# A two-layer decoder step on one core: the border between the layers in eight column steps, with the next layer's first tile among them

## The chip, the core and the metric

The kernel runs on one core of one Trainium2 chip. The metric is the device time of one execution in microseconds (us); lower is better. Before the change the median of three runs was 2055.4 us (2051.17 to 2055.42). The engines are named as the profile names them: PE is TensorE, PEld its weight loads, DVE VectorE, ACT ScalarE, POOL GpSimd, SP SyncE.

## The reference, cut to what matters

A prompt of 512 tokens behind 16 meta tokens and 8 sample tokens (536 rows in all) go through two layers of width 2048. Layer 0 has a pooling mixer and differential attention, layer 1 has gated linear attention with four heads. Each layer has the same frame:

```python
z = rms_norm(h, pre_g) @ w_in
...
h = h + rms_norm(mix @ w_out, post_g)
```

So the border between the layers needs, in this order: the last product of `mix @ w_out` of layer 0; the sum of squares over the whole row of 2048; the scaled residual `h`; its transposition, since PE wants the 2048 columns on the partitions; and `rms_norm(h, pre_g) @ w_in` of layer 1. The kernel multiplies `pre_g` into the transposed rows and applies the row's own `1/rms` only after the products, so the products of layer 1 needn't wait for the second norm.

Everything is float32. A product of two float32 matrices is made of three PE products of rounded parts ("hi" and "lo"): lo x hi, hi x lo, hi x hi.

## The kernel before, in words

**Engines and order.** Each engine has a program of its own, written out by hand, in order; semaphores tie them together. Weights stream through two raw buffers `wraw` (half a tile, 512 KB, each): SP loads a chunk (`load`, L451, and `out_load`, L531), ACT rounds it into `whi` (`split`, L663), POOL subtracts to get `wlo` (`lo`, L598), PE multiplies. SP may load a chunk only when POOL is done with the one two before it, and its program is in order: a wait in it holds up every load behind it.

**Layer 0** is four pairs of attention heads (`pair` on each engine), 24 weight chunks each. The programs of PE and DVE are written out for all four; those of SP (pairs 1 to 3, L528), POOL (L621) and ACT (pairs 0 to 2, L833) are loops of the chip with addresses in registers. Pages of the key and value caches are fetched by SP (`fetch`, L481), the last two samples' values by ACT (L773).

**Output products** (`out_stage` on each engine; once per layer). 32 chunks of weights; four column blocks of 512, each over eight chunks; per chunk PE makes 24 products for the four row tiles of 128 (`out_stage`, L1113). The last 24 rows (the tail) are made apart by narrow products straight from the raw weights (`tail_group`, L1098), copied to SBUF by DVE (L1785), and folded together by one product behind the block (L1140 to 1142). ACT squares every block's tile into a partial sum (`square`, L864), the tail last; DVE multiplies it by the post-norm weights `gain` (L1788, L1790). `gain` is loaded by SP behind chunk 9 (L543 to L547), after waits for ACT's last copy of the activations and for DVE. Before chunk 2 POOL has made the activations' residues (`lows`, L633) and the tails' copies (`mix_tails`, L624), and ACT the activations' copies (`mix_hi`, L711). When the products end, ACT first splits the first two chunks of layer 1 (L855), then squares the last block; DVE adds the sums (L1792), behind its multiply of the tail; ACT makes Ln and Exp (L861).

**The border** (L881 on ACT, L1320 on PE, L1797 to L1827 on DVE) goes in four steps of 512 columns. DVE makes five residuals, one for each row tile (L1800); PE transposes the 512 columns into four banks (`row_transposes`), ACT copies them with `pre_g` as the scale (L884), DVE makes the low parts (`low_rows`); PE multiplies the columns by 16 low-rank columns of `w_in` (`low_rank`, L1335). Behind the four steps ACT issues the stores of `h` (L888 to L890), squares `h` row by row over 2048 columns (L893), and makes the next norm; DVE puts it on diagonals (L1831), PE spreads it (`spread_rstd`), DVE copies it and scales the low-rank rows (L1841).

**Layer 1** is four heads (`head` on each engine), 24 chunks each: four value tiles, two of queries, two of keys, four of gates. The first chunk of the first value tile is multiplied ahead of PE's spread of the norm (L1440 to L1442), the second behind it. SP loads the decay weights `wa2` behind chunk 2 of a head, after a wait for the low-rank rows (L571 to L575). PE and the last head of ACT and DVE are written out; the first three heads of ACT (L1022) and DVE (L2020) and all heads of SP and POOL are loops.

## Time and profile before

| what | before |
|---|---|
| median of three runs | 2055.4 us (2051.17 to 2055.42) |
| the profiled execution: its own time | 2051.26 us |
| its span, first to last instruction | 2049.5 us |
| PE busy | 1950.3 us (95%), 13625 products |
| DVE, ACT, POOL busy | 732.8, 643.2, 899.9 us |
| mean granted clock of PE | 0.97 |

The span is what the profiler saw of one execution; its own time is 1.8 us longer, which lies around the span. A busy PE is not PE at its peak: products overlap, and the clock it is granted is not always the higher one. A row of the timeline gives the start from the beginning of the span, the duration, the engine and line, what is written from what, how many instructions were put together, and in brackets how long the engine had been idle and what released it. Nearly all PE work shows line 1036 or 1039, which are helpers, so its rows are told apart by their tiles.

### The profile page before, as it was taken

How to read it: one execution, taken by the hardware profiler on the slowest of the kernel's cores; microseconds unless marked ns; L12 is line 12 of the kernel's file. 1: busy time of each engine (PE TensorE's matmuls, PEld its weight loads, DVE VectorE, ACT ScalarE, POOL GpSimd, SP SyncE). 2: the span in 40 equal slices, each digit the busy share in tenths (PEclk: the TensorE clock that was granted, in tenths of full speed). 3: DMA queues.
4: the chain of work that ended last, by engine and by line, in shares of the span. 5: the costliest groups of instructions: out<-in, count | busy, mean ns of one | idle time of the engine just before them, and what ended most of it. 6: DMA issues, size and time to landing. Idle time of an engine off the chain costs nothing.

```text
span 2049.5 us, 36126 instructions
## 1 busy us (share of the span) xinstructions
PE 1950.3 (95%) x13625; PEld 1724.1 (84%) x13625; DVE 732.8 (36%) x1439; ACT 643.2 (31%) x1186; POOL 899.9 (44%) x1196
## 2 busy tenths in 40 slices
PE   6999999999999999999889999999999999989996
PEld 6998999898979887677679988988998899867774
DVE  5245235425442556000251354044305522550003
ACT  6132223222221234222243253334334423442221
POOL 2464447345624654544314333433442444354442
PEclk9999999999999999999999999999999899989998
DMA  5454345434533442352233543445244424522422
GB/s 169 118 154 134 96 117 145 142 87 126 149 114 106 130 140 89 103 168 83 75 119 95 153 145 93 118 119 183 65 125 153 133 77 125 177 83 99 170 91 111
DMA packets 300100, 250.05 MB, mean 122 GB/s; under 512 B 14855, under 2 KB 258968, under 8 KB 297016
## 3 DMA queue, kind: packets, MB, share of 16 engines
q1 hardware_dynamic: 260256, 189.06, 31.4%
q10 hardware_dynamic: 39688, 58.83, 8.7%
q8 instruction: 108, 1.77, 0.4%
q14 instruction: 48, 0.39, 0.1%
HBM read 215.73 MB, written 32.57 MB: 121 GB/s over the span
## 4 chain that ended last, share of the span: by engine, by line
issue 45%; POOL 33%; PE 19%; DVE 1%; DMA 0%; POOLq 0%; ACT 0%; DVEq 0%; SPq 0%; ACTq 0%
POOL wlo L603 28%; PE proj L1036 9%; PE score L1036 5%; POOL kv L618 4%; PE scratch L1036 4%; POOL xlo L637 1%; PE proj L1039 0%; DVE mix L1800 0%; DMA xin<-in_x_prompt 0%; POOLq L601 0%; POOL mtail L631 0%; PE score L1039 0%; PE scratch L1039 0%; DVEq L168 0%; DVE ytail L1800 0%
## 5 line engine op out<-in xcount | busy, mean ns | idle before, releaser
L603 POOL TENSOR_TENSOR wlo<-wraw,whi 128x256 fp32r<-128x256 f32 x1032 | 777.3, 786 | 1101.7 <-ACT whi L667 1101.2
L1036 PE MATMUL proj<-xhi,wlo 128*128 128x268 f32 (+1 forms) x3104 | 910.5, 293 | 8.2 <-POOL wlo L603 8.1
L1036 PE MATMUL proj<-xlo,whi 128*128 128x268 f32 (+1 forms) x3104 | 897.0, 289 | 0.0
L1036 PE MATMUL proj<-xhi,whi 128*128 128x268 f32 (+1 forms) x3104 | 896.4, 289 | 0.0
L1036 PEld LDWEIGHTS proj<-xhi,wlo 128*128 128x128 f32 x3104 | 596.7, 192 | 25.1 <-issue 19.7
L1036 PEld LDWEIGHTS proj<-xlo,whi 128*128 128x128 f32 x3104 | 596.7, 192 | 0.7
L1036 PEld LDWEIGHTS proj<-xhi,whi 128*128 128x128 f32 x3104 | 595.1, 192 | 0.0
L667 ACT ACTIVATE whi<-wraw 128x1024 fp32r<-128x1024 f32 x258 | 268.1, 1048 | 674.8 <-PE proj L1036 290.1
L1464 DVE TENSOR_TENSOR tz<-proj,rstd 128x536 f32<-128x536 f32 (+1 forms) x72 | 51.2, 712 | 327.7 <-PE proj L1036 327.2
L1036 PE MATMUL proj<-wlo,xhi 128*128 128x512 f32 x256 | 102.8, 402 | 0.0
L1036 PE MATMUL proj<-whi,xhi 128*128 128x512 f32 x256 | 101.1, 395 | 0.0
L1036 PE MATMUL proj<-whi,xlo 128*128 128x512 f32 x256 | 101.1, 395 | 0.0
L618 POOL TENSOR_TENSOR kv<-kv,qb 128x256 f32<-128x256 f32 x128 | 93.0, 756 | 5.6 <-DMA kv<-in_cache_k 4.4
L753 ACT ACTIVATE probw<-score,small 128x128 f32<-128x128 f32 (+3 forms) x64 | 33.2, 523 | 162.8 <-DVE small L1559 162.8
L1036 PE MATMUL score<-wlo,xhi 128*128 128x512 f32 x160 | 65.3, 408 | 5.3 <-POOL wlo L603 5.3
L1036 PEld LDWEIGHTS proj<-wlo,xhi 128*128 128x128 f32 x256 | 48.3, 189 | 24.4 <-issue 11.7
L1036 PE MATMUL score<-whi,xlo 128*128 128x512 f32 x160 | 64.7, 404 | 0.0
L1036 PE MATMUL score<-whi,xhi 128*128 128x512 f32 x160 | 64.5, 403 | 0.0
L1940 DVE SCALAR_TENSOR_TENSOR sst<-vb,gk,sst 128x512 f32<-128x512 f32 x64 | 57.0, 950 | 8.2 <-ACT sst L954 7.4
L1036 PEld LDWEIGHTS proj<-whi,xlo 128*128 128x128 f32 x256 | 48.2, 188 | 11.3
L1036 PEld LDWEIGHTS proj<-whi,xhi 128*128 128x128 f32 x256 | 48.4, 189 | 10.9
L1785 DVE COPY te<-proj 128x512 f32<-128x512 f32 x4 | 2.8, 692 | 135.5 <-DMA gain<-in_post_norm 77.5
(311 smaller groups left out, 2088.6 us busy)
## 6 DMA issues: line engine op xcount, KB each, us to landing
wraw<-in_w_in SPq DMA_DIRECT2D x192, 512.0 KB, 4.0
wraw<-in_w_out SPq DMA_DIRECT2D x64, 512.0 KB, 4.6
kv<-in_cache_k SPq DMA_DIRECT2D x128, 128.0 KB, 2.2
sst<-in_state_gla ACTq DMA_DIRECT2D x32, 512.0 KB, 5.1
out<-sst ACTq DMA_DIRECT2D x32, 512.0 KB, 3.6
kv<-in_cache_v SPq DMA_DIRECT2D x96, 128.0 KB, 2.2
vb<-v_sample_rows ACTq DMA_DIRECT2D x32, 256.0 KB, 5.5
qb<-q_sample_rows SPq DMA_DIRECT2D x32, 128.0 KB, 3.3
```

Source lines behind the costliest of these rows:

```text
L603: last = pool.tensor_tensor(wlo[:, slot, k:k + 2, 0:width], wraw[:, kc, k:k + 2, 0:width], whi[:, slot, k:k + 2, 0:width].bitcast(F32), AL ...
L618: last = pool.tensor_tensor(kv[b % 2][:, pg, :], kv[b % 2][:, pg, :], qb[b % 2][:], ALU.mult)
L637: pool.tensor_tensor(xlo[:, p, :], mix[:, ORDER[which][p], :], xhi[:, p, :].bitcast(F32), ALU.subtract).then_inc(s_xp, 1)
L667: act.activation(whi[:, 2 * par + kc, :, 0:width], wraw[:, kc, :, 0:width], ACT.Copy).then_inc(s_hi, 1)
L753: last = act.activation(prob[:, m, 0:n], score2[:, m, 0:n], ACT.Exp, bias=small[:, 2 + m:3 + m], scale=SCALE, accum_out=small[:, 4 + m:5 + m])
L1036: return pe.matmul(out, lhsT, rhs, start=start, stop=stop, skip_group_check=True)
L1464: dve.tensor_tensor(dst, src, root, ALU.mult).then_inc(s_evac, 1)
L1785: dve.tensor_copy(tef[:, 0:BLK], blk_bank(which, 5 * nb + TT)).then_inc(s_tcopy, 1)
L1940: last = dve.scalar_tensor_tensor(out=sst[i][:, j, :], in0=vb[i][:], scalar=gk[:, j, TP + b:TP + b + 1], in1=sst[i][:, j, :], op0=ALU.mult ...
```

## The change

1. **The border has eight steps of 256 columns.** Three banks (`row_bank`) take the transposes. In each step PE makes the low-rank products of the step before and also that step's products of the first value tile (`first_tile`), into the other `proj` buffer; its two chunks, 0 and 1 of the first head, are left out there.
2. **The next norm's squares** are made by ACT piece by piece inside the border (512 columns, 20 pieces, behind every second step) and added by DVE. The three fills of DVE (L1837 to L1839) move ahead of the next norm.
3. **The stores of `h`** move from ACT to SP, behind chunk 3 of the first head, with a wait for the last residual; `wa2` of the first head is loaded behind them, without the wait for the low-rank rows.
4. **The fold of the tail** moves ahead of the block's last 24 products; ACT squares the tail first; DVE's sum over the partial squares stands ahead of its last multiply; of the splits behind the products, those of the first value tile move behind Ln and Exp.
5. **Norm weights**: SP loads `gain` behind chunk 3 instead of chunk 9, and DVE waits for it only at its first multiply.
6. **Start of the output products**: POOL makes `wlo` of chunks 2 and 3 ahead of its last four activation residues, ACT splits them ahead of its last eight copies.
7. **Loops written out**: `pair` and `head` on SP, POOL, ACT and DVE.

The diff, cut to its core:

```diff
+        def row_bank(k):
+            return banks[(4, 6, 7)[k % 3]]
...
-            with sp.Fori(1, PAIRS) as g:
+            for g in range(1, PAIRS):
                 pair(g)
...
-                    if q == 9:
+                    if q == 3:
...
-            def head(s):
+            def head(s, first=False):
                 for c in range(24):
                     load(N_HEAD + c // 2 + 12 * s, c % 2, w_in1, head_col(c // 2, s))
-                    if c == 2:
+                    if c == 3 and first:
+
+                        sp.wait_ge(s_x1, 5 * STEPS)
+                        sp.dma_start(h_dram[TT, 0:TB], ytok[TT]).then_inc(s_hst_tail, 16)
+                        for tt in range(TT):
+                            sp.dma_start(h_dram[tt], ytok[tt]).then_inc(s_hst, 16)
+                        sp.wait_ge(s_hst_tail, 16)
+                        sp.dma_start(wa2[:], A["gla_wa2_1"][:, 0:GK]).then_inc(s_wa2, 16)
+                    if c == 2 and not first:
                         src = A["gla_wa2_1"][:, bass.ds((s + 1) * GK - GK, GK)]
-                        sp.wait_ge(s_lr, 1)
                         sp.wait_ge(*freed_back("head", "G11", s))
                         sp.dma_start(wa2[:], src).then_inc(s_wa2, 16)
...
+                for c in range(2 * n0 + 2, 2 * n0 + 4):
+                    lo(c, c % 4)
                 lows(which, (9, 11, 13, 15))
-                for c in range(2 * n0 + 2, 2 * n0 + 32):
+                for c in range(2 * n0 + 4, 2 * n0 + 32):
                     lo(c, c % 4)
...
+                for c in range(2 * n0 + 2, 2 * n0 + 4):
+                    split(c // 2, c % 2, c // 2 % 2)
                 for p, sig_ready in ready:
                     if sig_ready:
                         act.wait_ge(*sig_ready)
                     mix_hi(which, (p, p + 1))
-                for c in range(2 * n0 + 2, 2 * n0 + 32):
+                for c in range(2 * n0 + 4, 2 * n0 + 32):
...
-                    if q % 8 == 3 and q > 3:
-                        tail_square(which, q // 8 - 1)
-                for c in last:
-                    split(c // 2, c % 2, c // 2 % 2, RANK if c < 2 * N_LR + 2 else P)
+                for c in last[0:2]:
+                    split(c // 2, c % 2, c // 2 % 2, RANK)
                 block_squares(which, NBLK - 1)
-                tail_square(which, NBLK - 1)
                 act.wait_ge(s_rsum, which + 1)
                 act.wait_ge(s_ya, 5 * NBLK * (which + 1))
                 chain.link(act.activation(row_sum, row_sum, ACT.Ln, scale=1.0 / D, bias=eps))
                 act.activation(row_rs, row_sum, ACT.Exp, scale=-0.5).then_inc(s_rs, 1)
+                for c in last[2:]:
+                    split(c // 2, c % 2, c // 2 % 2)
...
+            for e in range(STEPS):
+                for k in (2 * e, 2 * e + 1):
...
-                    act.activation(xhi[:, k, 0:TT * P], banks[(2, 3, 6, 7)[k % 4]], ACT.Copy,
+                    act.activation(xhi[:, k, 0:TT * P], row_bank(k), ACT.Copy,
                                    scale=cols[:, PRE1 + k:PRE1 + k + 1]).then_inc(s_mh, 1)
-                act.wait_ge(s_gt, c + 1)
-                act.activation(xhi[:, 4 * c:4 * c + 4, TT * P:T], te4(c), ACT.Copy).then_inc(s_gth, 1)
-            act.dma_start(h_dram[TT, 0:TB], ytok[TT]).then_inc(s_hst_tail, 16)
-            for tt in range(TT):
-                act.dma_start(h_dram[tt], ytok[tt]).then_inc(s_hst, 16)
-            for tt in range(TT + 1):
-                w = P if tt < TT else TB
-                last = act.activation(hbuf[tt][0:w], ytok[tt][0:w], ACT.Square, accum_out=rsum[0:w, 30 + tt:31 + tt])
-            chain.link(last)
+                act.wait_ge(s_gt, e + 1)
+                act.activation(xhi[:, 2 * e:2 * e + 2, TT * P:T], te2(e), ACT.Copy).then_inc(s_gth, 1)
+                for t in range(TT + 1) if e % 2 else ():
+                    c = e // 2
+                    i, w = 5 * c + t, P if t < TT else TB
+                    if i >= 2:
+                        act.wait_ge(s_nsq, i - 1)
+                    act.activation((tzf, rstdf)[i % 2][0:w, 0:BLK], ytok[t][0:w, c * BLK:(c + 1) * BLK], ACT.Square,
+                                   accum_out=rsum[0:w, 40 + t * NBLK + c:41 + t * NBLK + c]).then_inc(s_nsq, 1)
...
+                        if k0 == KT - 2:
+                            pe.wait_ge(s_tcopy, NBLK * which + nb + 1)
+                            matmul(blk_bank(which, 5 * nb + TT)[0:TB, :], tfold, tef[:, 0:BLK]).then_inc(s_blk, 1)
...
-                    if grp % 4 == 3:
-                        pe.wait_ge(s_tcopy, NBLK * which + nb + 1)
-                        matmul(blk_bank(which, 5 * nb + TT)[0:TB, :], tfold, tef[:, 0:BLK]).then_inc(s_blk, 1)
...
+            def row_transposes(e):
+                pe.wait_ge(s_x1, 5 * e + 5)
+                if e:
+                    pe.wait_ge(s_gt, e)
+                for k in (2 * e, 2 * e + 1):
                     last = transpose(banks[5][:, k * TB:(k + 1) * TB], ytok[TT][:, k * P:(k + 1) * P])
                 last.then_inc(s_xtt, 1)
...
+                for k in (2 * e, 2 * e + 1):
+                    if k >= 3:
+                        pe.wait_ge(s_ml, k - 2)
+                    for t in range(TT):
+                        last = transpose(row_bank(k)[:, t * P:(t + 1) * P], ytok[t][:, k * P:(k + 1) * P])
+                    last.then_inc(s_xtr, 1)
...
+            def first_tile(e):
+
+                pe.wait_ge(s_lo, 2 * N_HEAD + 3 + e // 4)
+                for k in (2 * e, 2 * e + 1):
+                    for a in range(2):
+                        slot, x = 2 + k // HC, slice(a * TH, (a + 1) * TH)
+                        out = proj[1][:, a, 0:TH]
+                        matmul(out, wlo[:, slot, k % HC, :], xhi[:, k, x], start=k == 0, stop=False)
+                        matmul(out, whi[:, slot, k % HC, :], xlo[:, k, x], start=False, stop=False)
+                        last = matmul(out, whi[:, slot, k % HC, :], xhi[:, k, x], start=False, stop=k == KT - 1)
+                if e == STEPS - 1:
+                    last.then_inc(s_tile, 1)
+
             row_transposes(0)
-            pe.wait_ge(s_evac, N_LR + 1)
+            pe.wait_ge(s_evac, N_LR + 2)
             pe.wait_ge(s_lo, 2 * N_LR + 4)
-            for c in range(1, 4):
-                row_transposes(c)
-                low_rank(c - 1)
-            low_rank(3)
+            for e in range(1, STEPS):
+                row_transposes(e)
+                low_rank(e - 1)
+                first_tile(e - 1)
+            low_rank(STEPS - 1)
+            first_tile(STEPS - 1)
+            spread_rstd(2)
...
-                    chunk(n0 + c // 2, (1 + c // 2) % 2, c % 2, *((META, QH) if HEAD_TILES[c // 2][0] in "qg" else (0, TH)))
-                    if s == 0 and c == 0:
-                        spread_rstd(2)
+                    if s or c >= 2:
+                        chunk(n0 + c // 2, (1 + c // 2) % 2, c % 2, *((META, QH) if HEAD_TILES[c // 2][0] in "qg" else (0, TH)))
...
-                dve.wait_ge(s_gain, 16 * which + 16)
...
+                    dve.wait_ge(s_gain, 16 * which + 16)
+                    for i, t in enumerate((TT, 0, 1, 2, 3)):
+                        w = P if t < TT else TB
+                        dve.wait_ge(s_ya, 5 * (NBLK * which + nb) + i + 1)
+                        if nb == NBLK - 1 and t == TT - 1:
+                            dve.tensor_reduce(row_sum, blk_sum, AX.X, ALU.add).then_inc(s_rsum, 1)
+                        dve.tensor_tensor(ytok[t][:, f], blk_bank(which, 5 * nb + t)[0:w], gain[0:w, f], ALU.mult).then_inc(s_yd, 1)
...
-                    residual(t, slice(c * BLK, (c + 1) * BLK), s_x1)
-                if c:
-                    tail_gains(c - 1)
-                    low_rows(c - 1)
-            tail_gains(3)
-            low_rows(3)
+                    residual(t, slice(e * 2 * P, (e + 1) * 2 * P), s_x1)
+                if e:
+                    tail_gains(e - 1)
+                    low_rows(e - 1)
+            tail_gains(STEPS - 1)
+            low_rows(STEPS - 1)
+            dve.wait_ge(s_nsq, 20)
+            dve.tensor_reduce(next_sum, next_blk, AX.X, ALU.add).then_inc(s_nred, 1)
+            dve.wait_ge(s_hst_tail, 16)
+            dve.memset(st[:], 0.0)
+            dve.memset(gq[:], 0.0)
+            link(dve.memset(qd[:], 0.0))
             dve.wait_ge(s_next, 1)
```

## Rows read from the trace of the kernel before

**Rows 1.** The page's first part: busy us (share of the span) xinstructions of each engine

```profile
PE 1950.3 (95%) x13625; PEld 1724.1 (84%) x13625; DVE 732.8 (36%) x1439; ACT 643.2 (31%) x1186; POOL 899.9 (44%) x1196
```

**Rows 2.** Waits of PE: us in total, times, longest us

```profile
PE scratch L1036 <- DMA kv<-in_cache_v: 9.7, 11, 2.0
```

**Rows 3.** Timeline at layer 0's output products, POOL and PE: start, us, instruction [idle before <-releaser]

```profile
813.96 7.16 POOL L637 TENSOR_TENSOR xlo<-mix,xhi 128x536 fp32r<-128x536 f32 x4
...
821.07 5.54 POOL L603 TENSOR_TENSOR wlo<-wraw,whi 128x256 fp32r<-128x256 f32 x8
...
823.99 0.47 PE L1036 MATMUL score<-wlo,xhi 128*128 128x512 f32 x1 [2.30 <-POOL wlo L603]
```

**Rows 4.** Windows: busy us by engine, then granted PE clock, DMA share, GB/s

```profile
824.00:828.00 4.00, 4.00 (x17) 3.25 (x18) 0.00 (x0) 0.42 (x1) 2.61 (x4) 1.00 0.44 142
1020.00:1024.00 4.00, 3.30 (x16) 3.27 (x16) 3.96 (x6) 1.81 (x3) 0.00 (x0) 0.50 0.00 2
1024.00:1028.00 4.00, 2.81 (x20) 1.81 (x19) 3.23 (x7) 2.68 (x6) 0.00 (x0) 0.97 0.01 2
...
1844.00:1848.00 4.00, 4.00 (x13) 3.13 (x12) 0.00 (x0) 1.06 (x1) 1.66 (x4) 0.64 0.63 214
```

**Rows 5.** Timeline of PE at layer 1's output products

```profile
1842.08 0.47 PE L1036 MATMUL score<-wlo,xhi 128*128 128x512 f32 x1 [2.98 <-POOL wlo L603]
```

**Rows 6.** Timeline of PE in the layer border

```profile
1020.70 1.97 PE L1039 MATMUL proj<-both,mix 128*128 128x128 f32 x8 [9.16 <-DVE mix L1800]
...
1032.10 1.29 PE L1039 MATMUL proj<-both,mix 128*128 128x128 f32 x8
...
1038.37 1.28 PE L1039 MATMUL proj<-both,mix 128*128 128x128 f32 x8 [0.16 <-DVE xlo L1808]
```

**Rows 7.** Timeline of ACT and PE at the first head of layer 1

```profile
1055.98 0.21 ACT L896 ACTIVATE rsum<-rsum 128x5 f32<-128x5 f32 x1
...
1057.29 1.17 PE L1036 MATMUL score<-tz,both 128*128 128x268 f32 x4 [3.57 <-DVE tz L1831]
...
1069.07 1.06 ACT L667 ACTIVATE whi<-wraw 128x1024 fp32r<-128x1024 f32 x1 [0.57 <-DMA wraw<-in_w_in]
...
1076.55 1.33 PE L1039 MATMUL scratch<-both,tz 128*128 128x128 f32 x5 [2.32 <-DVE gb L1860]
```

**Rows 8.** Timeline of ACT behind the last products of layer 0

```profile
1010.67 2.00 ACT L667 ACTIVATE whi<-wraw 128x1024 fp32r<-128x1024 f32 x2 [8.18 <-PE proj L1036]
...
1014.86 0.57 ACT L870 ACTIVATE rstd<-proj 24x512 f32<-24x512 f32 x1
...
1016.46 0.30 ACT L861 ACTIVATE rsum<-rsum,stat 128x5 f32<-128x5 f32 x1 [0.94 <-DVE rsum L1792]
```

**Rows 9.** Timeline of DVE in the layer border

```profile
1015.68 0.67 DVE L1790 TENSOR_TENSOR ytail<-proj,gain 24x512 f32<-24x512 f32 x1
...
1017.26 0.74 DVE L1800 SCALAR_TENSOR_TENSOR ytail<-ytail,rsum,hbuf 24x512 f32<-24x512 f32 x1 [0.83 <-ACT rsum L862]
1017.93 2.72 DVE L1800 SCALAR_TENSOR_TENSOR mix<-mix,rsum,hbuf 128x512 f32<-128x512 f32 x4
...
1024.77 0.26 DVE L1818 TENSOR_TENSOR te<-score,cols 128x96 f32<-128x96 f32 x1 [0.81 <-PE score L1039]
1024.94 1.40 DVE L1808 SCALAR_TENSOR_TENSOR xlo<-proj,cols,xhi 128x512 fp32r<-128x512 f32 x2
```

**Rows 10.** Timeline of SP's issues: value pages of pair 0 and pair 1

```profile
185.08 15.56 SPq L487 DMA_DIRECT2D kv<-in_cache_v  x16
...
374.72 16.96 SPq L487 DMA_DIRECT2D kv<-in_cache_v  x16
```

**Rows 11.** Timeline of ACT from pair 0 to pair 1

```profile
226.93 2.00 ACT L667 ACTIVATE whi<-wraw 128x1024 fp32r<-128x1024 f32 x2
```

**Rows 12.** Issues of DMA: KB each, median us from issue to landing

```profile
wraw<-in_w_in SPq DMA_DIRECT2D x192, 512.0 KB, 4.0
...
gain<-in_post_norm SPq DMA_DIRECT2D x2, 1024.0 KB, 7.5
```

More of the change, by code:

```diff
@@ L619, in pair @@
                         last.then_inc(s_prod, 1)
-            with pool.Fori(0, PAIRS) as g:
+            for g in range(PAIRS):
                 pair(g)
@@ L652, in _ @@
                       range(2 * N_LR, 2 * N_LR + 4))
-            with pool.Fori(0, GH) as s:
+            for s in range(GH):
                 for c in range(24):
@@ L2018, in head @@
                 dve.wait_ge(s_head, s + 1)
-            with dve.Fori(0, GH - 1) as s:
-                chain.enter(s, HEAD_LINKS)
+            for s in range(GH - 1):
                 head(s)
-                chain.leave(GH - 1)
             head(GH - 1, final=True)
```

89 lines of the change are left out of this document (32 added, 57 removed).

## The prediction, made before the changed kernel was run

> **What bounds the kernel now.** The page's first part comes first: TensorE (PE) is busy for 95% of the span [rows 1], and its program has the same products before and after. So time can come from two places only: stretches in which PE waits, and stretches in which it runs at the lower of its two clocks (a granted clock of 0.50, 1.2 GHz, against 1.00, 2.4 GHz). The waits of PE were read next, then the timeline around each long one, then the granted clock there. Four places stand out, in the order of the kernel.
>
> In the four attention pairs PE waits 9.7 us, eleven times, for pages of the value cache [rows 2]. At the start of the output products of layer 0 it waits 2.30 us for a residue of the weights that POOL makes late [rows 3]; the clock stays high behind that [rows 4]. The same wait in layer 1 is 2.98 us [rows 5], and there the clock drops to 0.64 on average over 4 us [rows 4]. The largest is the layer border: 9.16 us before the first transposes [rows 6], with the clock at half until about 1024 [rows 4]; then 3.57 us for the norm of layer 1 and 2.32 us for a decay sum inside the first head [rows 7].
>
> The border's chain before 1020.70 reads so. The last product and the fold of the tail end near 1011.5. ACT first splits two weight chunks, 2.00 us, and only then squares the last block; the fifth square ends about 1015.5 [rows 8]. DVE's multiply of the tail, 0.67 us, still stands between that square and the sum of squares; ACT's Ln starts at 1016.46, and the first residual at 1017.26 [rows 8, 9]. Five residuals of 512 columns at some 0.67 us each follow, and PE starts.
>
> **The change, part by part.**
>
> *Loops written out.* PE's program was written out already. SP issues sixteen value pages in 15.56 us in pair 0, whose loads are written out, and in 16.96 us in pair 1, which is in the loop [rows 10]: 1.4 us for each of three pairs, 4.2 us at most, if PE waited for the last page each time. Nothing is the other end, since the last value pages come from ACT's queue. I take 1.5 us, nearer the lower end, because only part of the eleven waits is for pages from SP. At ACT's loop edge the split of the next pass starts at 226.93 with no idle time before it [rows 11]: I take nothing for ACT, POOL and DVE.
>
> The Trainium skill (Runtime: NRT & Kernel Launch, Instruction fetch mechanics) says that a taken branch whose target has left the small instruction window must wait for a fetch. By that rule each written-out loop would give more than I count; the edge above shows no such stall.
>
> *Start of the output products.* POOL now makes the residues of weight chunks 2 and 3 ahead of its last four activation residues, and ACT splits those chunks ahead of its last eight copies. Before, the four residues ran from 813.96 for 7.16 us, and the weight residues (5.54 us for two chunks, 2.8 each) began at 821.07 [rows 3]. Now the first is done by about 817, and PE asks for it at 821.7. The 2.30 us go whole. What is late next: the copies by 2.0 us, the four activation residues by 5.5 us; PE needs those with the fifth chunk, two chunks later, so this is covered. In layer 1 the same order takes away 2.98 us, and 0.36 of 4 us at the lower clock, 1.4 us [rows 4, 5]: 4.4 us together, 2.98 if the clock drops all the same.
>
> *Norm weights sooner.* SP is past this load earlier, but waits there, in order, for ACT's last copy; chunk 4 waits for PE's second tail group anyway, which comes later. The transfer of 7.5 us [rows 12] now meets the loads of chunks 4 and 5. If chunk 4 (4.0 us alone) only starts when the norm weights have landed, near 825, it is there at 829, and split and residue (1 and 2.8 us) bring it to 833, about when PE asks. So between nothing and 2 us for each layer; I take nothing, since transfers share the engines.
>
> *Fold in the last products.* The fold moves ahead of the last 24 products; PE's sum stays. The tail's square and three others are done before PE ends, the weight splits stand behind the norm, and the sum of squares stands ahead of the last multiply. So behind the last product (1011.6) come one square with its sum (0.7), then what stood between that multiply's end (1016.35) and the first residual (1017.26), 0.9 us [rows 8, 9]: the first residual at 1013.2, 4.0 us sooner. At the end of layer 1, where nothing is split, only the multiply goes: 0.6 us.
>
> *Eight steps with the first tile in them.* A residual of 256 columns costs between 0.34 us (half) and 0.68 us (all of it fixed) [rows 9]; I take 0.40: a 96-column row on the same engine is done in 0.26, so the fixed part is well under half of the 512-column one. PE starts at 1013.2 + 5 x 0.40 = 1015.2. From 1032.10 to 1038.37, less the wait, a step of before takes PE 6.1 us: 2.9 for transposes (two groups of 1.29 and the tail's) and 3.2 for 24 products [rows 6]. A new step has half of the transposes and again 24 products, 12 as before and 12 of the head's first tile: 4.7 us. DVE has five residuals, two low rows of 0.70 [rows 9] and two small operations, 3.7 us. So PE sets the pace, and the 96 products of the tile stand where waits were. Eight steps are 37.6 us; I add 2 us for a start at half clock, as before [rows 4], and half a microsecond for more changes between transposes and products: PE is through at 1055.3. At 0.68 DVE would need 5.1 us a step, 3 us more in all.
>
> The last transposes end 6.4 us earlier, 1048.9. ACT copies (1.2), squares the last five pieces (5 x 0.57, as the fifth at 1014.86 [rows 8]), and the sum, Ln and Exp (1.0) end at 1054.0, against 1056.2 before [rows 7]. PE's spread of the norm waits a microsecond or two, instead of 3.57.
>
> What then decides is the wait at 1076.55: it stood 7.5 us behind ACT's split at 1069.07, and that split waited for a weight load [rows 7] which SP held back behind the wait for the low-rank rows (L573). The decay load now comes behind the stores of the stream, which SP has issued by about 1047, long before the next load can go. So from 1054.0: 0.7 to the first split (1.1), its residue 2.8, the load 4.0 [rows 12], hand-overs 0.2: split at 1062.8, 6.2 us sooner, and so the end of the wait. PE's own side reaches this point earlier, even with two new waits of one to two microseconds. The h stores move from ACT's queue to SP's; ACT is 4 us freer in that.
>
> **Sum.** 1.5 (loops) + 2.3 + 4.4 (two starts) + 6.2 (border) + 0.6 (end) = 15.0 us. The profiled execution took 2051.3 us (span 2049.5), so 2036.3. The median of the runs shown is 2055.4, 4.1 above that execution; I forecast the median: 2040.
>
> **Rivals.**
> 1. *Half of it*, 0.17. The border ends DVE-bound (gain 3 us), the clock drops after the second start as before (2.98), the loops give nothing: 2.3 + 3.0 + 3 + 0.6 = 8.9 us, 2046.5. For it: many PE waits here are set by two engines at once. Against it: DVE has 1 us of room in each step.
> 2. *The loops give more*, 0.07. If SP or ACT stalls at each edge of its loop and comes late to its page fetches for it, the 9.7 us of waits for value pages [rows 2] could all go: 8.2 us beyond my 1.5, and 2032. It is what the rule of the Trainium skill named above would give here. Against it stands the edge [rows 11].
> 3. *It doesn't do what it says*, 0.05. The tile's products cost PE the same wherever they stand, so its place gives nothing by itself; if ACT's squares and the load chain set the first head's pace as before, the border gives 0, and contention of the norm weights takes 4 us of the rest: some 4 us less than before, 2051 or more.
> 4. *Slower*, 0.03. Place: the border. If PE waits in each of the eight steps, as long as the 2.98 us that cost the clock in layer 1, it stays at half clock throughout: 37.6 us more against the 15.0, 2078. It decides when DVE's step exceeds PE's by more than the 2.30 us that left the clock high, so at a residual of about 1.1 us. Against it: 0.68 is the upper bound, and the clock recovered to 0.97 in the same work between 1024 and 1028, with a wait of 0.16 us two steps on [rows 4, 6].
>
> **Numbers.** The forecast has 0.68. A measurement of this kernel tells 0.2%, about 4.1 us, from no change: cases 1, 2 and the forecast are faster, 3 about the same, 4 slower. Range: the border between 3 and 9 us, loops between 0 and 4.2, the starts between 5 and 7, and the 4 us between the execution profiled and the median: 2032 to 2048, which takes in 1 and 2.
>
> **What would show it.** The first residual some 4 us behind the end of the products; PE idle for about 3.6 us there instead of 9.16; transposes and products alternating without waits over 2 us; no wait for the weight residue at either start; the split that stood at 1069.07 about 6 us sooner relative to the end of the products; the PE waits for value pages near 8 us. Wrong would be: DVE without idle time in the border, PE at half clock past the second step, or a new PE wait for the weights of chunks 4 and 5.

## The result, and the profile after

Four runs of the changed kernel have a median of 2038.87 us (2033.90 to 2042.00); the kernel before has 2055.41 us beside them. The ratio is 0.9926, with a 95% interval of 0.9904 to 0.9947. The forecast was 2040, faster. The profiled execution is the slowest of the four: 2042.0 us of its own time, a span of 2040.1 us. So the two profiles lie 9.4 us apart, the two medians 16.5.

The first part of the page. PE has the same products and 1.5 us less busy time than in [rows 1].

```profile
PE 1948.8 (96%) x13625; PEld 1718.9 (84%) x13625; DVE 736.7 (36%) x1468; ACT 646.4 (32%) x1220; POOL 899.7 (44%) x1196
```

The waits of PE for value pages (us in all, times, longest), which answer to [rows 2]: 9.1 against 9.7.

```profile
PE scratch L1047 <- DMA kv<-in_cache_v: 9.1, 9, 2.0
```

The timeline of PE. The first two pairs of rows are the starts of the output products, which answer to [rows 3, 5]: the product behind the tail group (the narrow products of the last 24 rows) now follows it with no idle time. The rest is the border and the first head, for [rows 6, 7]; 1177.03 is the product of the first head that takes its values (`gv`), which serves as a mark below and is called the value product.

```profile
818.48 1.07 PE L1047 MATMUL proj<-wraw,mtail 128*32 128x512 f32 x8
819.47 0.50 PE L1047 MATMUL score<-wlo,xhi 128*128 128x512 f32 x1
...
1832.25 1.06 PE L1047 MATMUL proj<-wraw,mtail 128*32 128x512 f32 x8
1833.25 0.51 PE L1047 MATMUL score<-wlo,xhi 128*128 128x512 f32 x1
...
1013.57 0.41 PE L1050 MATMUL score<-both,ytail 24*128 24x24 f32 x2 [5.31 <-DVE mix L1825]
1018.12 0.38 PE L1050 MATMUL score<-both,ytail 24*128 24x24 f32 x2 [2.24 <-DVE te L1843]
1024.02 0.30 PE L1050 MATMUL score<-both,ytail 24*128 24x24 f32 x2
1028.24 0.30 PE L1050 MATMUL score<-both,ytail 24*128 24x24 f32 x2
1055.10 1.27 PE L1047 MATMUL score<-tz,both 128*128 128x268 f32 x4 [2.71 <-DVE tz L1862]
1058.02 2.12 PE L1047 MATMUL scratch<-lrT,wa 16*128 16x268 f32 x4 [1.65 <-DVEq L1870]
1068.81 0.77 PE L1050 MATMUL scratch<-both,tz 128*128 128x128 f32 x5 [0.21 <-DVE gb L1887]
1177.03 1.13 PE L1047 MATMUL scratch<-gv,kd 128*128 128x512 f32 x2 [0.85 <-ACT og L947]
```

The border's first wait is 5.31 us instead of 9.16, with a second of 2.24 behind it. A step is 4.2 us from the third on (1024.02 to 1028.24). Behind the border stand 2.71 and 1.65 us; the 2.32 us of [rows 7] are gone.

The timeline of DVE and POOL in the same stretch goes with PE's two waits; e4 below tests the cause. Four residuals of 256 columns take 1.65 us in the third step, but 3.11 and 3.54 us in the first two, while POOL subtracts (1010.78 to 1017.57). The low rows at 1017.90 stand just behind that. The five scaled diagonals at 1052.57 also lie beside POOL. The last row is ACT's split that stood at 1069.07 in [rows 7].

```profile
1010.00 0.47 DVE L1825 SCALAR_TENSOR_TENSOR ytail<-ytail,rsum,hbuf 24x256 f32<-24x256 f32 x1 [0.22 <-DVE mix L1817]
1010.41 3.11 DVE L1825 SCALAR_TENSOR_TENSOR mix<-mix,rsum,hbuf 128x256 f32<-128x256 f32 x4
1010.78 6.79 POOL L617 TENSOR_TENSOR wlo<-wraw,whi 128x256 fp32r<-128x256 f32 x8 [10.59 <-ACT whi L683]
1014.31 3.54 DVE L1825 SCALAR_TENSOR_TENSOR mix<-mix,rsum,hbuf 128x256 f32<-128x256 f32 x4
1017.90 0.73 DVE L1833 SCALAR_TENSOR_TENSOR xlo<-score,cols,xhi 128x512 fp32r<-128x512 f32 x1
1019.73 1.65 DVE L1825 SCALAR_TENSOR_TENSOR mix<-mix,rsum,hbuf 128x256 f32<-128x256 f32 x4
...
1052.57 2.47 DVE L1862 TENSOR_SCALAR tz<-both,rsum 128x128 f32<-128x128 f32 x5
1052.90 5.52 POOL L617 TENSOR_TENSOR wlo<-wraw,whi 128x256 fp32r<-128x256 f32 x8 [35.32 <-ACT whi L683]
...
1059.74 1.06 ACT L683 ACTIVATE whi<-wraw 128x1024 fp32r<-128x1024 f32 x1 [5.97 <-DMA wraw<-in_w_in]
```

The windows (busy us by engine, then granted clock, DMA share, GB/s), for [rows 4]: the clock is still below full between 1020 and 1024, at 0.76 on average (0.50 before), and it is full behind the start in layer 1, where it was 0.64.

```profile
1020.00:1024.00 4.00, 4.00 (x26) 3.88 (x24) 4.00 (x11) 3.42 (x10) 0.00 (x0) 0.76 0.22 66
...
1836.00:1840.00 4.00, 4.00 (x19) 3.24 (x18) 0.00 (x0) 2.11 (x2) 4.00 (x5) 1.00 0.51 190
```

Marks in both traces cut the span into stages. The products of layer 0 end where the border's first wait begins: 1020.70 - 9.16 = 1011.54 before, 1013.57 - 5.31 = 1008.26 after. The other marks are the value product of the first head and the product behind the last wait of the last head. In the kernel before they are these two rows:

```profile
1187.54 0.70 PE L1036 MATMUL scratch<-gv,kd 128*128 128x512 f32 x1 [0.85 <-ACT og L934]
...
1823.66 0.59 PE L1036 MATMUL scratch<-gq,both 128*128 128x8 f32 x2 [0.82 <-ACT ek L1018]
```

and in the changed kernel, beside 1177.03 above, this one:

```profile
1817.85 0.60 PE L1047 MATMUL scratch<-gq,both 128*128 128x8 f32 x2 [0.81 <-ACT ek L1031]
```

| stage | before | after | difference |
|---|---|---|---|
| to the first product behind the start, layer 0 | 824.0 | 819.5 | -4.5 |
| to the end of layer 0's products | 187.6 | 188.8 | +1.2 |
| border, to the value product of the first head | 176.0 | 168.8 | -7.2 |
| heads, to the last head's end | 636.1 | 640.8 | +4.7 |
| to the first product behind the start, layer 1 | 18.4 | 15.4 | -3.0 |
| to the end | 207.4 | 206.9 | -0.6 |

Two rows go the wrong way: the products of layer 0 got longer, and so did the heads, in which no product was changed. And the first row is not the start's alone: 2.1 of its 4.5 us lie ahead of the tail group (818.48 against 820.62). What lies ahead of that group differs from trace to trace: it begins at 818.5, 816.4, 820.4 and 810.3 us in the changed kernel, e9, e4 and e5, whose programs are the same up to there. A single trace therefore doesn't price a change in the pairs.

### The profile page after: what moved, and what is told of

Same layout as the page of the kernel before. It is cut to its first block, busy times and chain, and to the rows that moved or that the text cites. A ratio compares the mean times of both kernels' runs of the same rounds, so it can differ in the third digit from the quotient of the medians.

```text
span 2040.1 us, 34552 instructions
## 1 busy us (share of the span) xinstructions
PE 1948.8 (96%) x13625; PEld 1718.9 (84%) x13625; DVE 736.7 (36%) x1468; ACT 646.4 (32%) x1220; POOL 899.7 (44%) x1196
## 4 chain that ended last, share of the span: by engine, by line
PE 81%; DVE 5%; ACT 4%; POOL 2%; issue 2%; DMA 2%; SPq 2%; ACTq 1%; DVEq 0%; POOLq 0%
PE proj L1047 58%; PE scratch L1047 13%; PE score L1047 8%; PE scratch L1050 2%; POOL wlo L617 1%; DMA kv<-in_cache_v 1%; POOL kv L632 1%; SPq L493 1%; DVE mix L1825 1%; SPq L489 1%; DVE probw L1658 0%; ACT sst L967 0%; ACT whi L683 0%; DMA wraw<-in_w_out 0%; ACT ek L933 0%
```

## The experiments

Each run has its own median and its ratio to the kernel before, timed on the same chip in the same group.

**Loops alone (e1).** The kernel before, with all loops of `pair` and `head` written out:

```diff
-            with act.Fori(0, PAIRS - 1) as g:
-                chain.enter(g, PAIR_LINKS_ACT)
+            for g in range(PAIRS - 1):
                 pair(g)
-                chain.leave(PAIRS - 1)
...
```

> The kernel before with its loops over pairs and heads written out on SP, POOL, ACT and DVE, nothing else. Forecast of the prediction: 1.5 us less (0 to 4.2), the PE waits for value pages near 8 us in all instead of 9.7, the waits at the starts of the output products and at the border as before (2.30, 2.98, 9.16 us). Rival 2 (loops give more): 8 us less or more, with the waits for value pages nearly gone.

Measured: 2045.32 us, ratio 0.9975 (0.9963 to 0.9987), which is 5.1 us less (2.7 to 7.6). The forecast's 1.5 is too small, the rival's 8 too large. The waits for value pages are 7.1 us, where near 8 was expected. The border, which this kernel doesn't touch, also got shorter: the wait for the decay sum, 2.32 us in [rows 7], is 1.08. That asked for the next run.

**Loops of the heads alone (e11).** As e1, with the loops over pairs left standing.

> The kernel before with only the loops over the heads of layer 1 written out (SP, POOL, ACT, DVE); those over the pairs stand. Theory: about half of what all loops gave (5.1 us) comes from the entry into the head loops, where SP and ACT are late with the first head's weights: the PE wait of 2.32 us for the decay sum falls to about 1.1, less of the first head runs at half clock, and from the end of the products to the first wait for the value product it takes 173.3 us instead of 176.0: 2 to 3 us less than the kernel before. Rival: it all comes from the pairs, and this kernel is as slow as the kernel before.

Measured: 2051.85 us, ratio 0.9991 (0.9976 to 1.0006). In time that is not told from nothing, so the rival, that all of the gain comes from the pairs, stands there. In the trace the border is shorter: from the end of the products (1022.88 - 9.15 = 1013.73) to the value product it takes 173.3 us, 2.7 less. Here are SP, ACT and PE at the first head, first in the kernel before:

```profile
1056.85 1.06 ACT L667 ACTIVATE whi<-wraw 128x1024 fp32r<-128x1024 f32 x1 [0.67 <-ACT rsum L896]
...
1062.21 0.34 SPq L575 DMA_DIRECT2D wa<-in_gla_wa  x1
1062.85 1.35 SPq L455 DMA_DIRECT2D wraw<-in_w_in  x2
```

and then in e11:

```profile
1022.88 1.54 PE L1037 MATMUL proj<-both,mix 128*128 128x128 f32 x6 [9.15 <-DVE mix L1798]
...
1058.50 1.06 ACT L667 ACTIVATE whi<-wraw 128x1024 fp32r<-128x1024 f32 x1 [0.48 <-ACT rsum L896]
...
1063.82 0.33 SPq L575 DMA_DIRECT2D wa<-in_gla_wa  x1
1064.19 1.05 SPq L455 DMA_DIRECT2D wraw<-in_w_in  x2
1077.23 1.22 PE L1037 MATMUL scratch<-both,tz 128*128 128x128 f32 x5 [1.17 <-DVE gb L1858]
1187.01 1.13 PE L1034 MATMUL scratch<-gv,kd 128*128 128x512 f32 x2 [0.84 <-ACT og L934]
```

SP's gap between the two issues falls from 0.30 to 0.04 us (1062.85 less 1062.55, 1064.19 less 1064.15), ACT's ahead of its split from 0.67 to 0.48. These are small, but they stand in the chain that feeds the first head. PE's wait for the decay sum falls by 1.15 us, the one ahead of the spread of the norm by 0.2, and the rest of the 2.7 is clock. The two gaps are 0.45 us of this; what else moved in that chain was not taken apart.

But the heads behind the mark take it back. They last 638.4 us in e11 and 638.7 in e1, whose border stage is also 173.3 us, against 636.1 before. From the end of the products to the end of the last head it comes to 811.7 and 812.0 us against 812.1.

So the gain of e1 is to be looked for in the pairs. Over all traces, the waits for value pages are 8.1 to 10.7 us in the four kernels whose pair loops stand (mean 9.6) and 5.6 to 9.1 in the ten that have them written out (mean 7.2): 2.4 us less. The tail group at the start of layer 0's output products begins at 819.9 us on average in the four and at 815.5 in the ten, 4.4 sooner. That is an estimate, since single traces lie up to 10 us apart; what makes up the 2.0 us beyond the page waits was not found.

The Trainium skill (Runtime: NRT & Kernel Launch, Instruction fetch mechanics) has a taken branch wait for a fetch where the target is outside the window. The gaps of SP and ACT agree in sign; they can't tell a fetch from the work on addresses in registers, which also goes when a loop is written out.

**Start of the output products alone (e2).** The kernel before with part 6 of the change:

```diff
+                for c in range(2 * n0 + 2, 2 * n0 + 4):
+                    lo(c, c % 4)
                 lows(which, (9, 11, 13, 15))
-                for c in range(2 * n0 + 2, 2 * n0 + 32):
+                for c in range(2 * n0 + 4, 2 * n0 + 32):
                     lo(c, c % 4)
...
```

> The kernel before with only the new order at the start of the output products (residues of weight chunks 2 and 3 ahead of the last four activation residues on POOL, their splits ahead of the copies on ACT). Forecast: 6.7 us less; no PE wait for a weight residue at either start; granted clock 1.00 behind the second start; no new wait at the next chunks. Rival 1: the clock drops behind the second start all the same, or the four activation residues become late by themselves, and only 2 to 4 us are gained.

Measured: 2042.14 us, ratio 0.9959 (0.9946 to 0.9972), 8.4 us less (5.7 to 11.1). Neither start has a wait left, the clock behind the second is 1.00, and no wait comes at the next chunks. The forecast's 6.7 holds.

That the clock behind the second start belongs to the wait is not shown. In e1 and e11 the second start keeps its wait, 2.93 us in both, and the clock behind it is 1.00 all the same; in e8, with 2.97 us, it falls to 0.50 for a while as it does before. The stage from there to the end takes 205.8 and 205.6 us in e1 and e11 against 207.4 before. This is e11's window, to be read beside the last of [rows 4]:

```profile
1844.00:1848.00 4.00, 4.00 (x18) 3.23 (x19) 0.00 (x0) 0.45 (x1) 2.48 (x4) 1.00 0.50 143
```

**The border alone (e8).** The changed kernel with the loops standing and the old starts. SP's first head stays written out, since part 3 of the change needs it:

```diff
-            for s in range(1, GH):
+            with sp.Fori(1, GH) as s:
                 head(s)
...
-                for c in range(2 * n0 + 2, 2 * n0 + 4):
-                    lo(c, c % 4)
                 lows(which, (9, 11, 13, 15))
-                for c in range(2 * n0 + 4, 2 * n0 + 32):
+                for c in range(2 * n0 + 2, 2 * n0 + 32):
...
```

> The changed kernel with two parts undone: the loops stand again, and the starts of the output products have the old order. Left are the norm weights, the folds and the border in eight steps. The prediction's terms for these give 6.8 us less than the kernel before (6.2 and 0.6). Theory after the runs so far: from the end of the products of layer 0 to the first wait for the value product in the first head 6 to 7 us less (176.0 in the kernel before), the eight folds 2.6 us more, the end 0.7 less: 4 to 5 us less in all, with the waits for the weight residue at both starts (2.3 and 3.0) as before. Rival: since the loop edge at the first head is still there, its load comes late and the border gives only 3 us: 1 to 2 us less in all.

Measured: 2051.64 us, ratio 0.9995 (0.9981 to 1.0009), 1.0 us less (3.9 less to 1.8 more). Parts 1 to 5 of the change, the largest by far, give nothing that can be told by themselves, where 4 to 5 us were expected. The rival's 1 to 2 us fits the number, but not its reason, a border that gives only 3: the border itself did what the theory said:

```profile
823.95 0.47 PE L1047 MATMUL score<-wlo,xhi 128*128 128x512 f32 x1 [2.27 <-POOL wlo L617]
...
1018.02 0.40 PE L1050 MATMUL score<-both,ytail 24*128 24x24 f32 x2 [5.32 <-DVE mix L1825]
...
1182.22 1.12 PE L1047 MATMUL scratch<-gv,kd 128*128 128x512 f32 x2 [0.85 <-ACT og L945]
```

From 1018.02 - 5.32 = 1012.70 to 1182.22 it takes 169.5 us, 6.5 less than 176.0. But from 823.95 to 1012.70 it takes 188.75, 1.2 more than the 187.55 of before: that is the folds. The heads take 1.7 us more than before, and the stretch behind them 1.0 more. Together the trace is 2.6 us shorter.

**The folds (e3).** In the kernel before, a fold and the tail products behind it alternate on PE, as the timeline shows. From the fold to the next full-height product it takes 1.83 us (911.97 - 910.14), where a tail group without a fold takes 0.99 (819.47 - 818.48 above). So a fold costs 0.84 us here, not nothing, as the expectation below has it:

```profile
910.14 0.61 PE L1036 MATMUL score<-te,both 128*24 128x512 f32 x1
910.16 0.63 PE L1036 MATMUL scratch<-wraw,mtail 128*32 128x512 f32 x3
910.59 0.59 PE L1036 MATMUL score<-te,both 128*24 128x512 f32 x1
910.61 1.43 PE L1036 MATMUL scratch<-wraw,mtail 128*32 128x512 f32 x5
911.97 0.50 PE L1036 MATMUL proj<-wlo,xhi 128*128 128x512 f32 x1
```

In the changed kernel it stands alone among full-height products. It takes 0.97 us there, and some 0.1 us more is lost at each of its ends: the starts are 0.32 and 0.34 us apart where the products change, 0.23 between two full-height ones. That makes 1.17, so the new place costs 0.33 more:

```profile
900.42 1.04 PE L1047 MATMUL score<-te,both 128*24 128x512 f32 x2
901.39 0.51 PE L1047 MATMUL proj<-wlo,xhi 128*128 128x512 f32 x1
```

The edit puts three of the four folds back, and with them the old order of squares and multiplies:

```diff
-                        if k0 == KT - 2:
+                        if k0 == KT - 2 and nb == NBLK - 1:
                             pe.wait_ge(s_tcopy, NBLK * which + nb + 1)
                             matmul(blk_bank(which, 5 * nb + TT)[0:TB, :], tfold, tef[:, 0:BLK]).then_inc(s_blk, 1)
...
+                    if grp % 4 == 3 and nb < NBLK - 1:
+                        pe.wait_ge(s_tcopy, NBLK * which + nb + 1)
+                        matmul(blk_bank(which, 5 * nb + TT)[0:TB, :], tfold, tef[:, 0:BLK]).then_inc(s_blk, 1)
```

> The changed kernel with the folds of the first three column blocks of each output stage put back behind the last product of their block, where the kernel before has them; the fold of the last block stays ahead. Theory: the kernel before runs these folds beside the tail products that follow, so that they cost nothing, and the new place costs 0.33 us of PE time each (a block takes 50.5 us instead of 50.2). Expected: blocks of 50.2 us again, 1.5 to 2 us less than the changed kernel, the border as in the changed kernel. Rival: the longer blocks are due to later loads or residues, not to the folds; blocks stay at 50.5 and the time does not change.

Measured: 2034.07 us, ratio 0.9921 (0.9903 to 0.9940). The changed kernel itself, run again in the next group (e9), has 2037.05 us, 0.9927 (0.9909 to 0.9944). The medians don't tell 2 us apart; the trace does. Fold and tail products alternate again, the products of layer 0 take 187.8 us from the first one behind the start to their end instead of 188.8, three folds at 0.33 each, and the stage from the last head to the end is 220.6 us instead of 222.3.

> The changed kernel itself, unaltered, so that the others of this group have it beside them on the same chip. Expected 12 to 16 us under the kernel before: the waits and clock losses that differ between the two traces add up to 13 us, the four first runs of each to 16.5.

So e9 gives 15.0 us less than the kernel before (11.5 to 18.7), where 12 to 16 was expected.

**POOL out of the way (e4).**

```diff
-                for c in last:
-                    lo(c, c % 4, RANK if c < 2 * N_LR + 2 else P)
+                for c in last[0:2]:
+                    lo(c, c % 4, RANK)
+                if which == 0:
+                    pool.wait_ge(s_x1, 10)
+                for c in last[2:]:
+                    lo(c, c % 4)
```

> The changed kernel, but POOL makes the two residues of the head's first tile only when the residuals of the first two column steps are done. Theory: DVE's residuals of steps 0 and 1 are slow (3.11 and 3.54 us for four, where later steps take 1.65) because POOL subtracts on the same memory at that time. Expected: four residuals take 1.65 us in steps 0 and 1 and are slow in step 2, where POOL now works; PE's first wait 3.6 to 4 us instead of 5.31, the second (2.24 us) under 1; 2 to 4 us less than the changed kernel. Rival: they are slow because of their place (first uses of the residual rows, ACT's splits), and stay slow with POOL idle; no gain.

Measured: 2035.75 us, ratio 0.9927 (0.9910 to 0.9945): not told from the changed kernel in time. The timeline decides the question of the cause:

```profile
1012.37 1.65 DVE L1829 SCALAR_TENSOR_TENSOR mix<-mix,rsum,hbuf 128x256 f32<-128x256 f32 x4
...
1016.08 6.29 POOL L617 TENSOR_TENSOR wlo<-wraw,whi 128x256 fp32r<-128x256 f32 x8 [13.91 <-DVE mix L1829]
1016.29 0.75 DVE L1837 SCALAR_TENSOR_TENSOR xlo<-score,cols,xhi 128x512 fp32r<-128x512 f32 x1 [0.16 <-ACT xhi L900]
1019.08 3.57 DVE L1829 SCALAR_TENSOR_TENSOR mix<-mix,rsum,hbuf 128x256 f32<-128x256 f32 x4
...
1014.08 0.40 PE L1054 MATMUL score<-both,ytail 24*128 24x24 f32 x2 [3.86 <-DVE mix L1829]
1022.91 0.28 PE L1054 MATMUL score<-both,ytail 24*128 24x24 f32 x2 [0.42 <-DVE te L1847]
```

The slow residuals moved with POOL, from the first two steps to the third (3.57), and PE's waits fell from 5.31 and 2.24 to 3.86 and 0.42, as expected. The low rows (0.75, one input from PSUM) are not slowed beside the same POOL work. From the end of the products to the value product it is 167.6 us, 1.1 less than in the first trace of the changed kernel and 2.3 less than in e9's. That is at most the lower end of the 2 to 4 us expected, though the two waits fell by 3.3 together; where the rest went was not taken apart (PE's first steps run at a clock of 0.50 in both).

**Zeroings ahead of the sum (e5).**

```diff
-            dve.wait_ge(s_nsq, 20)
-            dve.tensor_reduce(next_sum, next_blk, AX.X, ALU.add).then_inc(s_nred, 1)
             dve.wait_ge(s_hst_tail, 16)
             dve.memset(st[:], 0.0)
             dve.memset(gq[:], 0.0)
             link(dve.memset(qd[:], 0.0))
+            dve.wait_ge(s_nsq, 20)
+            dve.tensor_reduce(next_sum, next_blk, AX.X, ALU.add).then_inc(s_nred, 1)
```

> The changed kernel with DVE's three zeroings (1.8 us) moved ahead of the sum of squares of the next norm, where DVE has waited 2.23 us for ACT. Theory: the scaled diagonals start behind the Exp, 1.2 us sooner, and are done before POOL's weight residue slows DVE (five take 1.0 us instead of 2.47), so the PE wait for them falls from 2.71 us to under 0.8, and 2 to 3 us are gained against the changed kernel. Rival: the weights of the first head become the next thing that is late and PE waits for them instead; under 1 us.

Measured: 2036.09 us, ratio 0.9917 (0.9903 to 0.9931): not told from the changed kernel's 2037.05 in the same group, where 2 to 3 us less were expected. The diagonals take 1.02 us, 0.6 behind Exp, and the wait of 2.71 us is gone. But the wait behind it grew:

```profile
1043.04 1.02 DVE L1862 TENSOR_SCALAR tz<-both,rsum 128x128 f32<-128x128 f32 x5 [0.60 <-ACT rsum L909]
...
1048.38 2.12 PE L1047 MATMUL scratch<-lrT,wa 16*128 16x268 f32 x4 [3.09 <-DMA wa<-in_gla_wa]
```

Neither the theory nor the rival had named what is late next: not the weights of the tile but the 16 KB of decay weights, which SP issues behind 4 MB of stores. From the end of the products to the value product it is 167.8 us, 1.0 less than in the first trace of the changed kernel and 2.2 less than in e9's.

**All three together (e7), and the two small loads ahead of the stores (e10, e12).**

> The changed kernel with three alterations together: first three folds of each output stage back behind their block, POOL's two residues behind the first two column steps, and the zeroings ahead of the sum. Sum of what the traces show of each: 2.6 (folds), 1.1 to 3 (border's first steps), 2 to 3 (zeroings): 6 to 8 us less than the changed kernel. Rival: the gains at the border run into one next wait, the first head's weights, and only 3 to 4 us are left.

Measured: 2028.01 us, ratio 0.9886 (0.9871 to 0.9902). Its interval lies apart from that of the changed kernel in the same group, and the median is 9.0 us lower, where 6 to 8 were expected. The border stage is 165.3 us. This version beats both kernels.

```diff
                         sp.wait_ge(s_hst_tail, 16)
                         sp.dma_start(wa2[:], A["gla_wa2_1"][:, 0:GK]).then_inc(s_wa2, 16)
+                        sp.dma_start(lower[:], A["lower"]).then_inc(s_c1, 16)
                         for tt in range(TT):
                             sp.dma_start(h_dram[tt], ytok[tt]).then_inc(s_hst, 16)
```

The first two lines, moved ahead of the stores, are e10; the added one is e12, which drops the load of the triangle (`lower`, a constant of 68 KB) from ACT's queue.

> The kernel with the three alterations, and SP issues the load of the decay weights ahead of the four large stores of the stream, behind which it took 10.7 us to land. Expected: the PE wait of 3.10 us for these weights falls to the 1.6 us that the low-rank rows take, 1 to 1.5 us less. Rival: DVE waits at this place for another load (the triangle, until 1045.84 in the kernel with three alterations), and the gain is lost in the next wait; no difference.

Measured: 2029.96 us, ratio 0.9893 (0.9871 to 0.9916), the same as e7. The decay weights land 1.6 us after their issue instead of 10.7, and PE's wait falls to 1.65. But DVE now waits 3.25 us for the triangle, behind the later stores, and PE gets a wait of 1.01 us for the decay sum: the rival. The heads take 636.2 us in this trace, against 638.7 in e7's, with no edit there.

> As the kernel before it (three alterations, decay weights ahead of the large stores), and the load of the triangle too is issued ahead of those stores, on SP, instead of behind them on ACT's queue. Theory: these two small loads were late only because of the stores; DVE's wait of 3.25 us for the triangle goes, and with it PE's wait of 1.01 us for the decay sum; 1 to 2 us less than the kernel with three alterations, so some 10 us under the changed kernel and 24 under the kernel before. Rival: the stores end later by as much and hold back the loads of the first head's next weights; no difference to the kernel with three alterations.

Measured: 2027.48 us, ratio 0.9874 (0.9856 to 0.9892), again not told from e7. The triangle lands in 1.9 us, but PE's wait for the decay sum is 2.91 us. ACT's split of the third chunk stands ahead of the decays, as in [rows 7], and waits for its load: from SP's issue to that split it takes 4.9 us (1047.20 to 1052.14), in e7 3.8 (1044.79 to 1048.60). The theory fell here, and it is as the rival said: the two small loads are no longer late, but the weights now are. That the stores hold them back is likely by the order alone; no run shows it apart.

**Norm weights late again (e6).** `if q == 3` is `if q == 9` again.

> The changed kernel with the load of the norm weights back behind the tenth weight load of each output stage. The prediction took nothing for this part: no difference to the changed kernel (within 2 us), and no PE wait for the weights of chunks 4 and 5 in either. Rival: DVE now waits for the norm weights only behind the copy of the tail, so that either place is covered; also no difference. A loss over 2 us would show that the earlier place did matter.

Measured: 2036.55 us, ratio 0.9927 (0.9906 to 0.9948), the same as the changed kernel. The part is worth nothing either way, as was forecast.

## Why the prediction was right, and where it was not

The time came out 1.1 us from the forecast, but two of its terms were wrong by several us in opposite directions. That they nearly cancel is luck. By the runs:

| term | forecast | measured alone |
|---|---|---|
| loops | -1.5 | -5.1 (e1) |
| starts | -6.7 | -8.4 (e2) |
| border, norm, folds, end | -6.8 | -1.0 (e8) |
| sum | -15.0 | -14.5; the whole kernel -15.0 (e9) |

- **Loops: the step that failed.** The term priced SP's value pages alone; "I take nothing for ACT, POOL and DVE" was read at one edge, that of the pairs, where ACT has work waiting. The runs have 5.1 us (2.7 to 7.6), over the bound of 4.2, though not clear of it. The page waits fell by 2.4 us on average, near the forecast; the pairs as a whole got shorter by about 4.4 (the estimate above), and what makes up the difference was not found. At the first head ACT and SP do stand in the one chain that feeds PE: the border stage got 2.7 us shorter in e1 and e11, but the heads behind it gave 2.6 and 2.3 of that back. Rival 2 had the direction right and the way wrong: in e1 the page waits are still 7.1 us.
- **The overlap.** What the loops take off the border stage is not had a second time in the full kernel: with this border, the stage is 169.5 us in e8, where only SP's first head is written out, and 168.8 to 170.0 in the four traces with all loops written out and nothing else altered there (the changed kernel, e9, e6, e3). The sum of -14.5 is no proof that the parts are independent, since each is known only to some 2.5 us either way.
- **Starts: right, the clock in part by luck.** Both waits went whole, and nothing was late next. Of the 6.7 us, 1.4 were for the clock behind the second start; it stayed up here, but it also did in e1 and e11, with the wait in place. So the 2.98 us that "cost the clock" in the prediction and in its rival 4 don't decide it.
- **Border: the size of its own stage was right (6.2 forecast; 6.5 in e8, 7.2 and 6.0 in the two traces of the full kernel), by steps that were not all.** The first residual came 1.74 us behind the products' end (1010.00 - 1008.26) against 5.72 before, 4.0 sooner as worked out. The load came sooner too: ACT's split stands 51.5 us behind the end of the products (1059.74) instead of 57.5 (1069.07), some 6 us sooner as forecast, and the decay wait at 1076.55 went from 2.32 us to 0.21. But PE's first wait was to be 3.6 us and was 5.31, with 2.24 behind it: "I take 0.40" for a residual holds from the third step on (1.65 for four), but not beside POOL, where it is 0.78 to 0.89, above the upper bound of 0.68. The bound was made from rows in which POOL had no work of that kind beside a residual, and moving the splits behind Exp put it there. A step costs 4.2 us of PE, not 4.7, which paid for it: six steps at 0.5 less are 3.0 us. That, too, is luck.
- **The fold: the step that failed most quietly.** "PE's sum stays" was taken from the count of products. The count does stay, but the old place shares the tail group's two changes of shape, and the new place has two of its own: 1.17 us a fold instead of 0.84. The prediction's "two places only" had left out this third one, busy PE time that depends on what stands beside it. That is 0.33 us a block, 1.2 us in layer 0 (188.8 against 187.6) and more in layer 1, where e3 gets 1.7 back with three folds.
- **End and norm weights: right.** The first residual at the end comes 1.6 us behind the last product instead of 2.2, so 0.6 us; the norm weights give nothing (e6).
- **Rivals.** The border did not become DVE-bound for long (rival 1), the kernel is not slower (rival 4), and the clock did recover past the second step. Rival 3, that the border gives nothing, is closest for parts 1 to 5 in time (e8), but by another cause: its gain at the border was real and was spent on the folds and in the heads.

What stays open is the heads. Without any change in their products they take 636.1 and 636.0 us in the traces of before and e2, 636.2 and 636.1 in e10 and e12, and 637.8 to 640.8 in the other ten. Those ten have the new border or the loops of the heads written out, but e10 and e12 have both, so neither decides it by itself. What the time goes into can be seen in the first head. These windows begin 36 us behind the value product, before and then after; PE is busy in all of them, at a clock of 0.76 and 0.81 before and 0.50 after:

```profile
1223.54:1227.54 4.00, 4.00 (x15) 2.75 (x15) 2.52 (x4) 3.59 (x7) 2.29 (x3) 0.76 0.10 33
1227.54:1231.54 4.00, 4.00 (x30) 4.00 (x29) 3.30 (x4) 2.02 (x4) 1.47 (x2) 0.81 0.20 23
```

```profile
1213.03:1217.03 4.00, 4.00 (x8) 1.60 (x7) 0.75 (x1) 3.31 (x6) 2.07 (x4) 0.50 0.21 70
1217.03:1221.03 4.00, 4.00 (x18) 3.82 (x18) 3.71 (x6) 2.23 (x4) 0.72 (x2) 0.50 0.48 113
```

In e10 the same two windows are at 0.77 and 0.81 again. Over all heads PE is busy for 622.68 us after and 619.06 before, with the same 4697 products. Why the change moves the clock there was not found. It takes back some 2 us of the gain, and the 4.7 of the first trace are part of why that execution is the slowest of its four.

## What to carry to other kernels

A duration is good only beside the same neighbours: before a step is moved, look at what the other engine on the same memory does at its new place, and what the moved product used to run beside. An edge of a loop is to be priced where its engine stands in the chain that feeds the bound engine, not at the edge that is easiest to read; and a gain at one wait is to be followed to the end of the kernel, since stages behind it can give it back. When a wait is taken away at a border, read the whole queue of what is late next, small loads behind large stores included.

## What the runs showed of the hardware

- **DVE and POOL on SBUF.** Residuals, whose two tensor inputs lie in SBUF, take 0.41 us each alone and 0.78 to 0.89 beside POOL's subtractions, which slow too (6.79 us for eight against 5.5). Low rows, with one input in PSUM, take 0.73 to 0.75 in both cases. Five diagonals, each with one tensor input in SBUF, take 2.47 against 1.02. The Trainium skill (SBUF — State Buffer, Who interferes with whom) says that a DVE instruction with two SBUF inputs contends with a GpSimd instruction that reads SBUF, one with at most one doesn't outside certain modes, and that the two share one pair of ports as a lock. The times of residuals and low rows agree; the diagonals would have to run in one of those modes, which no run here shows, and none shows whether it is a lock.
- **What a 24-row product costs depends on its neighbours.** A fold of two such products costs 0.84 us where it alternates with tail products of 32 rows, and 1.17 us alone among full-height products.
- **A small load was late behind large stores issued ahead of it:** 16 KB on the same queue took 10.7 us behind 4 MB, and 1.6 us ahead of them. Another queue didn't help: 68 KB on ACT's queue took 5.4 to 7.0 us behind the same stores, and 1.9 us ahead of them on SP's.
